# GLA states: gates projected first and values last, decays among the projections, sample outputs in four column tiles, sample states in two row tiles

## The chip, the core and the metric

The kernel runs on one core of one Trainium2 chip. Its engines are TensorE (PE, matmuls and the loads of their weights), VectorE (DVE), ScalarE (ACT) and GpSimd (POOL); SyncE (SP) issues most DMAs. Each engine works through its own list in order, and the engines meet at semaphores. The metric is the device time of one execution in microseconds (us).

## The reference

One inference step of a trunk of two layers on 512 prompt rows and 8 samples of 8 new rows (64 rows). Layer 0 mixes by attention, layer 1 by gated linear attention (GLA); each then has a feed-forward network with a short convolution. The change is in the mixer of layer 1, with 4 heads, dk = 128, dv = 256:

```python
def step(S, inp):                       # one chunk of one head
    qc, kc, vc, gc = inp
    b = jnp.cumsum(gc, axis=2)
    o_inter = jnp.einsum('bhtd,bhdv->bhtv', qc * jnp.exp(b), S)
    att = jnp.einsum('bhtd,bhsd,bhtsd->bhts', qc, kc, decay)      # decay = exp(b_t - b_s), s <= t
    o = o_inter + jnp.einsum('bhts,bhsv->bhtv', att, vc)
    S = jnp.exp(b_last) * S + jnp.einsum('bhsd,bhsv->bhdv', kc * jnp.exp(b_last - b), vc)
    return S, o
h = x @ w_in                            # q | k | v | r
on = o * lax.rsqrt(jnp.mean(jnp.square(o), -1, keepdims=True) + RMS_EPS) * norm_g
y = (on * jax.nn.silu(r)) @ w_out
```

The prompt starts from a zero state, each sample from its own (128 x 256 per head, read from HBM and written back). The outputs are y and the states.

## The kernel before, in words

The 576 rows are five tiles: four of 128 prompt rows (t = 0 to 3) and one of the 64 sample rows (t = 4). Each weight is loaded in units of 512 KB by SP into `raw`; ACT rounds a unit (`split_hi`, L1138), DVE takes the rest (`split_lo`, L1475), and PE forms three products per weight tile (`project`, L669 and L680 for the sample tile). In layer 1, q and k come first, feature-major, with the decays' cumulative sums `g_b`; then eight units `gla_vr` project the values v (units 0 to 3) and then the gates r (units 4 to 7), each unit in five steps, one per tile. Beside these 40 steps run 32 level steps (4 heads x 8 levels, L1026 and L1032 on PE), which build the decayed scores `att[h]`: DVE makes differences (`differences`), ACT their exponentials (`decay`), DVE the decayed q and k (`decayed`), PE the products (`level_products`) and DVE places them by mask (`placed`, L1857). DVE works one level step ahead of PE.

Then comes the stage of states, head by head, behind the last projection:

- ACT takes the exponentials of the sums (`decays_of`), DVE scales keys and queries (`prepare`, L1904, L1905), PE turns the scaled keys in five transposes (`turn_keys_of`, L650), ACT copies them out. For head 0 this is done after the last projection, for head h + 1 during head h. ACT applies SiLU to all five gate tiles (L1432) ahead of head 0's squares.
- PE forms four prompt state increments (L1059, 128 rows), then four prompt outputs: `att` times values (L1074) and, from tile 1 on, scaled queries times the state before (L1078). DVE carries the state (`bring_state`, L1934 and L1941), ACT squares each output (L1441) and DVE multiplies it by the gate (`gate_out`, L1926).
- The samples: one product of scores and values (L1088), then eight matmuls that add each sample's queries times its state. The queries of sample s stand in a block of 64 columns that is zero outside its own eight (`g_qz`), so each of the eight takes 64 columns of the array and all add into the same 64 rows of PSUM (L1090). Then eight state increments (L1059, 64 rows): the keys are zeroed outside the sample (`g_kz`, L1916). DVE adds each to the decayed old state (L1978).
- POOL stores the states (L2084, L2086). The sample states of the heads take turns in two buffers: SP loads head 2's when head 0's has been stored, head 3's when head 1's has.
- In the last head, DVE takes the reciprocal of all roots and then norms and scales every piece (`normed`, L1949), two tiles before its last four state updates and three between the y tiles; PE turns y (`turn_y`, L650), ACT and DVE copy it out in two parts (`take_x` L1124, `x_los` L1482), and PE starts the output projection (`gla_out`, L669).

The order on each engine is written out by hand. What holds PE in the loop of heads are these waits:

```python
            turn_keys_of(0)
            for h in range(GH):
                pe.wait_ge(turned_out, BATCH_GLA + 2 * h + 2)
                ...
                for s in range(SEQS):
                    mm = pe.matmul(place, g_qz[par][:, s, :], g_sst[par][:, s, :], start=False, stop=s == SEQS - 1)
                mm.then_inc(go_done, 1)
                for s in range(SEQS):
                    if s == 4 and h + 1 < GH:
                        turn_keys_of(h + 1)
                    state_product(h, PQ + s, g_kz[par][0:NS, s, :], vv)
```

## Time and profile before

| | us |
|---|---|
| median of 3 runs (lowest, highest) | 1608.63 (1607.99, 1610.58) |
| the profiled execution | 1606.65 |
| its span, first to last instruction | 1604.9 |
| PE busy in the span (share) | 1508.3 (94%) |
| DVE busy | 920.0 (57%) |
| ACT busy | 553.4 (34%) |
| POOL busy | 57.1 (4%) |
| granted TensorE clock, mean | 0.971 |

### The profile page before, as it was taken

Reading aid. Unit: us, or ns where it says so; the run is one execution under the profiler, and the core shown is the slowest. Engines: PE = TensorE matmul, PEld = TensorE weight load, DVE = VectorE, ACT = ScalarE, POOL = GpSimd, SP = SyncE. Lnnn points to the kernel's source line nnn. Section 1 sums busy time; section 2 is a strip of 40 time slices with the busy share of each in tenths; the row PEclk is TensorE's granted clock in tenths of the full one; section 3 lists DMA queues with packets and bytes.
Section 4 is the critical chain, followed back from the end, with each engine's and each line's share of the span. In section 5 each row is a group of like instructions: output and inputs, shape, how many; then the busy total and the mean of one; then the engine's idle time right before and its main releaser. Section 6 shows DMA issues by size and latency. Waiting matters only on the chain.

```text
span 1604.9 us, 24203 instructions
## 1 busy us (share of the span) xinstructions
PE 1508.3 (94%) x9372; PEld 1331.2 (83%) x9372; DVE 920.0 (57%) x1738; ACT 553.4 (34%) x1030; POOL 57.1 (4%) x90
## 2 busy tenths in 40 slices
PE   6999897889999999999799999899899999999995
PEld 5888675669999999878698888668799999998784
DVE  2654253377666666554721776575676666665545
ACT  3222276324333333332225332521243333333321
POOL 0002200010000000000100000000100000000000
PEclk9999999989999999999899999999799999999998
DMA  5225456622223321422211211442022333214211
GB/s 174 102 99 163 115 203 232 171 73 80 79 82 90 88 80 52 129 79 92 78 55 53 79 53 53 136 150 80 27 80 79 84 90 87 79 52 128 79 66 59
DMA packets 153215, 153.56 MB, mean 96 GB/s; under 512 B 12014, under 2 KB 122734, under 8 KB 152910
## 3 DMA queue, kind: packets, MB, share of 16 engines
q1 hardware_dynamic: 149210, 139.47, 28.1%
q0 software_dynamic: 3936, 13.14, 2.6%
q8 instruction: 47, 0.77, 0.2%
q14 instruction: 22, 0.18, 0.0%
HBM read 140.76 MB, written 21.91 MB: 101 GB/s over the span
## 4 chain that ended last, share of the span: by engine, by line
PE 85%; DVE 7%; ACT 3%; SPq 2%; issue 2%; DMA 1%; POOL 0%; ACTq 0%; DVEq 0%; POOLq 0%
PE ps L669 69%; PE ps L680 4%; PE ps L650 4%; PE ps L1026 1%; DVE x_reg L1684 1%; PE ps L737 1%; PE ps L1059 1%; PE ps L771 1%; SPq L522 1%; PE ps L1090 1%; DVE x_reg L1688 1%; DVE w_lo L1475 1%; ACT w_hi L1138 1%; PE ps L947 1%; DVE x_reg L1666 1%
## 5 line engine op out<-in xcount | busy, mean ns | idle before, releaser
L669 PE MATMUL ps<-xh_reg,w_hi 128*128 128x288 f32 x1552 | 465.4, 300 | 8.2 <-DVE xl_reg L1482 8.2
L669 PE MATMUL ps<-xl_reg,w_hi 128*128 128x288 f32 x1552 | 460.8, 297 | 0.0
L669 PE MATMUL ps<-xh_reg,w_lo 128*128 128x288 f32 x1552 | 460.8, 297 | 0.0
L669 PE MATMUL ps<-w_hi,xh_reg 128*128 128x512 f32 x768 | 308.2, 401 | 6.9 <-DVE xl_reg L1726 3.4
L669 PEld LDWEIGHTS ps<-xh_reg,w_hi 128*128 128x128 f32 x1552 | 295.1, 190 | 10.5 <-DVE xl_reg L1482 5.4
L669 PE MATMUL ps<-w_hi,xl_reg 128*128 128x512 f32 x768 | 302.2, 394 | 0.0
L669 PE MATMUL ps<-w_lo,xh_reg 128*128 128x512 f32 x768 | 302.1, 393 | 0.0
L669 PEld LDWEIGHTS ps<-xl_reg,w_hi 128*128 128x128 f32 x1552 | 295.3, 190 | 0.0
L669 PEld LDWEIGHTS ps<-xh_reg,w_lo 128*128 128x128 f32 x1552 | 294.9, 190 | 0.0
L1475 DVE TENSOR_TENSOR w_lo<-raw,w_hi 128x2048 fp32r<-128x2048 f32 (+1 forms) x52 | 113.7, 2186 | 259.1 <-ACT w_hi L1138 259.1
L669 PEld LDWEIGHTS ps<-w_hi,xh_reg 128*128 128x128 f32 x768 | 146.3, 191 | 39.0 <-issue 7.2
L1138 ACT ACTIVATE w_hi<-raw 128x2048 fp32r<-128x2048 f32 (+1 forms) x55 | 100.8, 1833 | 223.2 <-PE ps L680 215.0
L669 PEld LDWEIGHTS ps<-w_hi,xl_reg 128*128 128x128 f32 x768 | 145.9, 190 | 31.4
L1761 DVE TENSOR_SCALAR arena<-arena 128x512 f32<-128x512 f32 (+1 forms) x176 | 67.7, 427 | 179.3 <-ACT arena L1297 179.3
L1763 DVE SCALAR_TENSOR_TENSOR arena<-arena 128x512 f32<-128x512 f32 x352 | 166.8, 515 | 6.3
L669 PEld LDWEIGHTS ps<-w_lo,xh_reg 128*128 128x128 f32 x768 | 146.3, 191 | 28.9
L1296 ACT ACTIVATE arena<-ps 128x224 f32<-128x224 f32 x88 | 31.5, 358 | 239.4 <-PE ps L669 239.4
L1745 DVE TENSOR_TENSOR w_lo<-raw,w_hi 128x2048 fp32r<-128x2048 f32 x44 | 100.5, 2284 | 3.3 <-ACT w_hi L1283 3.1
L1283 ACT ACTIVATE w_hi<-raw 128x2048 fp32r<-128x2048 f32 x44 | 83.7, 1902 | 0.1
L680 PE MATMUL ps<-w_hi,xh_reg 128*128 128x512 f32 x192 | 75.8, 395 | 1.3 <-DVE x_reg L1670 1.3
L650 PE MATMUL ps<-ident,x_reg 128*128 128x128 f32 (+1 forms) x232 | 40.9, 335 | 38.1 <-DVE xl_reg L1482 12.2
L1294 ACT ACTIVATE arena<-ps 128x288 f32<-128x288 f32 x88 | 36.0, 412 | 112.7 <-PE ps L669 112.7
(188 smaller groups left out, 1530.5 us busy)
## 6 DMA issues: line engine op xcount, KB each, us to landing
raw<-in_ffn_w_up SPq DMA_DIRECT2D x88, 512.0 KB, 5.0
raw<-in_ffn_w_down SPq DMA_DIRECT2D x40, 512.0 KB, 4.6
raw<-in_attn_w_in SPq DMA_DIRECT2D x24, 512.0 KB, 4.8
raw<-in_gla_w_in SPq DMA_DIRECT2D x24, 512.0 KB, 4.6
out_swa_s<-in_state_swa_kv SPq DMA_DIRECT2D x2, 3968.0 KB
x_reg<-in_x_prompt SPq DMA_DIRECT2D x8, 512.0 KB, 7.1
raw<-in_gla_w_out SPq DMA_DIRECT2D x8, 512.0 KB, 4.7
out_swa_p<-arena POOLq DMA_DIRECT2D x18, 128.0 KB, 3.0
```

Of the source, the lines that this page charges most:

```text
L522: sp.dma_start(values_of[s][:, b:b + GROUP_BLOCKS[g], :] if g < 3 else values_of[s][:, b, :], src).then_inc(v_cached[s // 4], 16)
L650: last = pe.transpose(ps[0:cols, bank, col:col + rows], src, ident[0:rows, 0:rows])
L669: mm = pe.matmul(out, lhs(i, a), rhs(i, b), start=first and i == 0 and a + b == 0, stop=last and i == ks - 1 and a == 1)
L680: mm = pe.matmul(ps[:, t, :], xTh[:, k0 + i, NP:SLOT], w[b][:, i, :], start=first and i + b == 0, stop=last and i == kn - 1 and b == 1)
L1138: act.activation(w_hi[:, n % 2, 0:a], raw[:, n % 2, 0:a], ACT.Copy).then_inc(hi_done, 1)
L1283: act.activation(w_hi[:, slot, :], raw[:, slot, :], ACT.Copy).then_inc(hi_done, 1)
L1294: act.activation(ext[:, u, v, 2:2 + SPLIT], ps[:, m, 0:SPLIT], ACT.Copy).then_inc(ext_ready, 1)
L1296: act.activation(ext[:, u, v, 2 + SPLIT:2 + NP], ps[:, m, 0:PRE], ACT.Copy)
L1475: dve.tensor_tensor(w_lo[:, n % 2, 0:a], raw[:, n % 2, 0:a], w_hi[:, n % 2, 0:a].bitcast(F32), ALU.subtract).then_inc(lo_done, 1)
L1745: dve.tensor_tensor(w_lo[:, slot, :], raw[:, slot, :], w_hi[:, slot, :].bitcast(F32), ALU.subtract).then_inc(lo_done, 1)
L1761: ins = dve.tensor_scalar(y, e, w, fj[:, u, v, SIDE - 1:SIDE], ALU.mult, ALU.add)
L1763: ins = dve.scalar_tensor_tensor(y, e, w, y, ALU.mult, ALU.add)
```

## The change

The projection order becomes gates first, values last. With that, ACT applies SiLU during the last unit. For heads 0 to 2, the differences, exponentials and scalings (in place, in `g_k` and `g_q`) and the key transposes go in between the level steps, one head after its eight levels; the transposes are in two parts, three and two. Head 3's scalings stand after the last level, followed by a product of each gate tile with the norm's weights (`norm_gate`); its transposes stand behind head 0's prompt states on PE. The decays at chunk ends are taken once for all heads (`ends`).

A sample's queries now stand in a block of 32 columns (four samples share one), and the eight sample outputs go to four column tiles of the array and so to four groups of 32 PSUM rows, two matmuls each; ACT copies the lower 64 rows (`o_low`), DVE adds the upper ones and multiplies by the gate. A state increment reads only 32 rows of keys and values, in row tile 0 or 1, which alternate and write to alternating banks; PSUM places are handed out in groups of four. Roots and reciprocals are taken per head, and the scaling by them is on ACT (`scale_by_root`), a head later. The sample states have places of their own except head 2, which follows head 0. The low part of the second `gla_out` unit goes from DVE to POOL.

```diff
+KEYS_AT = [(h_ + 1) * (NLEV + 1) for h_ in range(GH)]
+LAST_ENDS_AT = LEVEL_STEPS - 5
...
+        g_state = [cut(arena, 24592 + i * GV, GV) for i in range(2)]
         g_sst = [x.rearrange("p (s n) -> p s n", s=SEQS)
-                 for x in (cut(gla_side, 7296, SEQS * GV), cut(arena, 21560, SEQS * GV))]
-        squares = cut(gla_side, 9344, GV)
+                 for x in (cut(arena, 21560, SEQS * GV), cut(gla_side, 7680, SEQS * GV), cut(arena, 21560, SEQS * GV),
+                           cut(arena, 17152, SEQS * GV))]
...
-                k0, kn, c0, cn = c % 2 * 4, 4, (c // 2 + (2 if kind == "gla_vr" else 0)) * HALF, HALF
+                k0, kn, c0, cn = c % 2 * 4, 4, ((c // 2 + 2) % 4 + 2 if kind == "gla_vr" else c // 2) * HALF, HALF
...
             for h in range(GH):
                 if h == 0:
+                    sp.wait_ge(lev_prod, GH * LEV_ALL)
+                elif h == 1:
                     sp.wait_ge(steps, STEPS_BEFORE[out])
-                elif h == 1:
-                    sp.wait_ge(lev_prod, GH * LEV_ALL)
+                elif h == 2:
+                    sp.wait_ge(s_state_out[0], 16)
                 else:
-                    sp.wait_ge(s_state_out[h % 2], 16)
-                sp.dma_start(g_sst[h % 2], io["state_gla"][0, :, h].rearrange("s d v -> d s v")).then_inc(gla_state_in[h % 2], 16)
+                    sp.wait_ge(go_done, 2 * NTILE)
+                sp.dma_start(g_sst[h], io["state_gla"][0, :, h].rearrange("s d v -> d s v")).then_inc(gla_state_in[h], 16)
                 if h == 1:
                     load_unit(out + 2)
                     load_unit(out + 3)
...
+            def turn_keys_of(h, part):
...
+                if part == 0:
+                    for c in range(3):
+                        mm = pe.transpose(ps[:, 7, NS + c * P:NS + (c + 1) * P], g_k[:, h, c * P:(c + 1) * P], ident[:, :])
+                else:
+                    pe.transpose(ps[:, 7, NS:NS + P], g_k[:, h, 3 * P:NP], ident[:, :])
+                    mm = pe.transpose(ps[0:NS, 7, NS + P:NS + 2 * P], g_k[:, h, NP:NT], ident[:, :])
+                mm.then_inc(keys_turned, 1)
...
+                    for h in range(GH - 1):
+                        for part in range(2):
+                            if m == KEYS_AT[h] + 4 + part:
+                                turn_keys_of(h, part)
+            pe.wait_ge(tok_read, 3 * NTILE + PQ)
             pe.wait_ge(lev_read, GH * LEV_ALL)
...
             for h in range(GH):
                 par = h % 2
-                pe.wait_ge(turned_out, BATCH_GLA + 2 * h + 2)
+                pe.wait_ge(keys_taken, 2 * h + 2)
                 for c in range(PQ):
-                    state_product(h, c, g_kt[par][:, c, :], g_v[:, c, h * GV:(h + 1) * GV])
+                    state_product(h, c, keys_of(h)[:, c, :], g_v[:, c, h * GV:(h + 1) * GV])
+                if h == 0:
+                    turn_keys_of(GH - 1, 0)
+                    turn_keys_of(GH - 1, 1)
+                pe.wait_ge(q_scaled, h + 1)
                 for c in range(PQ):
                     n = h * NTILE + c
-                    if n >= 3:
-                        pe.wait_ge(go_read, n - 2)
...
                     place = head_out_place(n, P)
                     mm = pe.matmul(place, att[h][:, c * P:(c + 1) * P], g_v[:, c, h * GV:(h + 1) * GV],
                                    start=True, stop=c == 0)
                     if c >= 1:
                         pe.wait_ge(gs_read, h * HEAD_STEPS + c)
-                        mm = pe.matmul(place, g_qb[par][:, c * P:(c + 1) * P], g_state[(c - 1) % 2],
+                        mm = pe.matmul(place, g_q[:, h, c * P:(c + 1) * P], g_state[(c - 1) % 2],
                                        start=False, stop=True)
                     mm.then_inc(go_done, 1)
...
-                pe.matmul(place, att[h][0:NS, NP:NT], vv, start=True, stop=False)
-                for s in range(SEQS):
-                    mm = pe.matmul(place, g_qz[par][:, s, :], g_sst[par][:, s, :], start=False, stop=s == SEQS - 1)
+                pe.matmul(place[0:NS], att[h][0:NS, NP:NT], vv, start=True, stop=False, skip_group_check=True)
+                for b in range(2):
+                    for s in (b, 4 + b, 2 + b, 6 + b):
+                        at = 32 * (s // 4) + NS * (s % 4 // 2)
+                        mm = pe.matmul(place[at:at + 32], g_qz[par][:, s, :], g_sst[h][:, s, :], start=at >= NS and b == 0, stop=b == 1,
+                                       skip_group_check=True, tile_position=(0, at))
                 mm.then_inc(go_done, 1)
-                for s in range(SEQS):
-                    if s == 4 and h + 1 < GH:
-                        turn_keys_of(h + 1)
-                    state_product(h, PQ + s, g_kz[par][0:NS, s, :], vv)
+                pe.wait_ge(kz_ready, h + 1)
+                for i in range(PQ, HEAD_STEPS):
+                    s = sample_of(i)
+                    rows = slice(32 * (s // 4), 32 * (s // 4) + 32)
+                    state_product(h, i, g_kz[par][rows, s % 4, :], vv[rows])
...
+                    for h in range(GH):
+                        if m == (KEYS_AT[h] if h < GH - 1 else LAST_ENDS_AT + 1):
+                            decays_of(h)
+                        for part in range(2):
+                            if h < GH - 1 and m == KEYS_AT[h] + 5 + part:
+                                take_keys_of(h, part)
...
+                    if i == 7 and t < 3:
+                        if t == 0:
+                            act.wait_ge(tok_read, 3 * NTILE)
+                        for tile in range(2 * t, min(2 * t + 2, NTILE)):
+                            silu_of(tile)
...
+                for t in range(PQ):
+                    act.wait_ge(go_done, h * NTILE + t + 1)
+                    square(h, t, head_out_place(h * NTILE + t, P))
+                act.wait_ge(go_done, (h + 1) * NTILE)
+                if h:
+                    act.wait_ge(go_read, h * NTILE)
+                act.activation(o_sum_of[0:NS, :], head_out_place(h * NTILE + PQ, NS), ACT.Copy).then_inc(o_low, 1)
+                if h:
+                    scale_by_root(h - 1)
+                else:
                     split_hi(UNIT_NO[("gla_out", 1)])
...
+                act.wait_ge(o_summed, h + 1)
+                square(h, PQ, o_sum_of[0:NS, :])
+                act.wait_ge(sq_done, sq.n)
+                act.activation(g_rs[:, :, h], g_ss[:, :, h], ACT.Sqrt, bias=eps_ln[:, 1:2], scale=1.0 / GV).then_inc(roots, 1)
+            scale_by_root(GH - 1)
+            act.wait_ge(gs_done, GH * HEAD_STEPS // 2)
...
+            def scale_keys(h):
+                dve.wait_ge(lev_prod, levels_done((h + 1) * (NLEV + 1) - 1))
+                dve.wait_ge(decays, 2 * h + 2)
+                dve.tensor_tensor(g_k[:, h], g_k[:, h], to_end, ALU.mult).then_inc(keys_ready, 1)
+            def scale_queries(h):
+                dve.tensor_tensor(g_q[:, h], g_q[:, h], from_start, ALU.mult).then_inc(q_scaled, 1)
+            def norm_gate(t):
+                n = TILES[t][1]
+                dve.wait_ge(r_gate, t + 1)
+                r = g_r[0:n, t, :].rearrange("p (h v) -> p h v", h=GH)
+                dve.tensor_tensor(r, r, g_norm[0:n, :].rearrange("p (o v) -> p o v", o=1).to_broadcast([n, GH, GV]),
+                                  ALU.mult).then_inc(r_normed, 1)
...
+                        if m == (KEYS_AT[h] - 1 if h < GH - 1 else LAST_ENDS_AT):
+                            end_differences(h)
+                        if h < GH - 1 and m == KEYS_AT[h] + 1:
+                            scale_keys(h)
+                        if h < GH - 1 and m == KEYS_AT[h] + 2:
+                            scale_queries(h)
             placed(LEVEL_STEPS - 1)
+            scale_keys(GH - 1)
+            scale_queries(GH - 1)
+            for t in range(NTILE):
+                norm_gate(t)
...
-                dve.wait_ge(sq_done, n + 1)
                 if h == 0:
-                    dve.wait_ge(r_gate, t + 1)
+                    dve.wait_ge(r_normed, t + 1)
                 r = g_r[0:rows, t, h * GV:(h + 1) * GV]
-                dve.tensor_tensor(r, head_out_place(n, rows), r, ALU.mult).then_inc(go_read, 1)
+                if t < PQ:
+                    dve.wait_ge(sq_done, n + 1)
+                    dve.tensor_tensor(r, head_out_place(n, rows), r, ALU.mult).then_inc(go_read, 1)
+                    return
+                dve.wait_ge(o_low, h + 1)
+                dve.tensor_tensor(o_sum_of[0:NS, :], head_out_place(n, P)[NS:P], o_sum_of[0:NS, :], ALU.add).then_inc(o_summed, 1)
+                dve.wait_ge(o_summed, h + 1)
+                dve.tensor_tensor(r, o_sum_of[0:NS, :], r, ALU.mult).then_inc(go_read, 1)
+            def place_samples(h):
...
+                for a in range(2):
+                    ins = dve.tensor_copy(g_qz_own[par][a], g_q[:, h, NP + 32 * a:NP + 32 * a + 32].rearrange("p (s t) -> p s t", s=4))
+                ins.then_inc(qz_own, 1)
+                dve.wait_ge(keys_taken, 2 * h + 2)
+                dve.tensor_tensor(g_kz[par][0:NS, :, :], sample_keys_of(h).rearrange("p (s d) -> p s d", s=1).to_broadcast([NS, 4, P]),
+                                  row_in_four.rearrange("p (s o) -> p s o", o=1).to_broadcast([NS, 4, P]), ALU.mult).then_inc(kz_ready, 1)
...
             add_low_half_of_vr(3)
-            prepare_samples(0)
+            place_samples(0)
             for h in range(GH):
                 for c in range(PQ):
                     bring_state(h, c)
                     if c >= 1:
                         gate_out(h, c - 1)
+                gate_out(h, 3)
                 if h + 1 < GH:
-                    prepare(h + 1)
-                gate_out(h, 3)
+                    place_samples(h + 1)
                 gate_out(h, 4)
...
+                def root(h):
+                    dve.wait_ge(roots, h + 1)
+                    dve.reciprocal(g_rs[:, :, h], g_rs[:, :, h]).then_inc(rs_ready, 1)
+                if h == GH - 1:
+                    root(h)
+                for i in range(PQ, HEAD_STEPS):
+                    n, s = h * HEAD_STEPS + i, sample_of(i)
+                    if i == PQ:
                         dve.wait_ge(go_done, (h + 1) * NTILE)
+                    dve.wait_ge(gs_done, 2 * (n // 4 + 1))
+                    state = g_sst[h][:, s, :]
+                    dve.scalar_tensor_tensor(state, state, ends[:, h, PQ + s:PQ + s + 1], state_place(n),
                                              ALU.mult, ALU.add).then_inc(gs_read, 1)
...
-                if h == 0:
-                    split_lo(UNIT_NO[("gla_out", 1)])
+                if h < GH - 1:
+                    root(h)
+            dve.wait_ge(s_state_out[1], 16)
...
                 pool.dma_start(io["gla_p"][0, 0, h], g_state[1]).then_inc(p_state_out, 16)
+                if h == 0:
+                    n = UNIT_NO[("gla_out", 1)]
+                    pool.wait_ge(hi_done, n + 1)
+                    pool.wait_ge(lo_done, n)
+                    pool.tensor_tensor(w_lo[:, n % 2, 0:UNIT], raw[:, n % 2, 0:UNIT], w_hi[:, n % 2, 0:UNIT].bitcast(F32),
+                                       ALU.subtract).then_inc(lo_done, 1)
                 pool.wait_ge(gs_read, (h + 1) * HEAD_STEPS)
-                pool.dma_start(io["gla_s"][0, :, h].rearrange("s d v -> d s v"), g_sst[h % 2]).then_inc(s_state_out[h % 2], 16)
+                pool.dma_start(io["gla_s"][0, :, h].rearrange("s d v -> d s v"), g_sst[h]).then_inc(s_state_out[h], 16)
```

## Rows read from the trace of the kernel before

**Rows 1.** The page, chain that ended last: shares of the span by engine.

```profile
PE 85%; DVE 7%; ACT 3%; SPq 2%; issue 2%; DMA 1%; POOL 0%; ACTq 0%; DVEq 0%; POOLq 0%
```

**Rows 2.** Windows: stretch, length, busy time (instructions) per engine, PEclk, DMA share, GB/s.

```profile
970.00:1012.60 42.60, 42.04 (x230) 35.50 (x228) 23.59 (x47) 13.06 (x18) 0.00 (x0) 1.00 0.08 26
1017.00:1020.00 3.00, 3.00 (x7) 2.46 (x8) 1.98 (x3) 2.99 (x3) 0.00 (x0) 0.50 1.10 353
295.00:300.00 5.00, 5.00 (x58) 2.71 (x58) 0.03 (x1) 1.07 (x4) 0.00 (x0) 1.00 0.04 11
```

**Rows 3.** PE's timeline, end of projections to output projection: start, length, line, shapes, records [idle].

```profile
1012.42 0.39 PE L680 MATMUL ps<-w_lo,xh_reg 128*128 128x512 f32 x1
1015.32 1.01 PE L650 MATMUL ps<-ident,gla_side 128*128 128x128 f32 x5 [2.50 <-DVE arena L1538]
1082.51 0.78 PE L669 MATMUL ps<-w_hi,xh_reg 128*128 128x512 f32 x1
```

**Rows 4.** Chain of waits in the stage of states: start, length, what (records).

```profile
1018.21 4.84 ACT arena L1432 x5
1051.45 0.86 PE ps L1074 x4
1054.47 0.57 PE ps L1088 x2
1055.04 3.60 PE ps L1090 x16
1058.64 1.92 PE ps L1059 x8
1061.26 3.85 PE ps L1059 x16
1065.10 0.86 PE ps L1074 x4
1075.34 3.26 DVE arena L1949 x8
```

**Rows 5.** PE's timeline in layer 0's attention: column tiles, next line, row tiles.

```profile
295.41 1.07 PE L845 MATMUL ps<-v_cache_reg,arena 128*32 128x256 f32 x16
296.41 1.56 PE L840 MATMUL ps<-arena 64*128 64x256 f32 x6
200.07 1.99 PE L737 MATMUL ps<-arena 64*128 64x512 f32 x8
```

**Rows 6.** DVE in the stage: line, shapes, count | busy, mean ns | idle before.

```profile
L1978 DVE SCALAR_TENSOR_TENSOR gla_side<-gla_side,arena,ps 128x256 f32<-128x256 f32 x16 | 6.8, 477 | 2.2 <-PE ps L1059 2.2
L1926 DVE TENSOR_TENSOR arena<-ps,arena 128x256 f32<-128x256 f32 x16 | 6.7, 422 | 3.8 <-ACT gla_side L1441 3.8
L1916 DVE TENSOR_TENSOR gla_side<-gla_side,arena 64x1024 f32<-64x1024 f32 x4 | 4.8, 1212 | 1.7 <-ACT gla_side L1124 1.7
```

**Rows 7.** DVE's timeline: the first instruction behind its last level.

```profile
1008.58 0.81 DVE L1895 TENSOR_TENSOR arena<-arena 128x512 f32<-128x512 f32 x2
```

**Rows 8.** ACT from the last unit on, columns as in 6.

```profile
L1441 ACT ACTIVATE gla_side<-ps 128x256 f32<-128x256 f32 x16 | 6.1, 379 | 14.0 <-PE ps L1074 9.0 <-PE ps L1078 4.8
L1138 ACT ACTIVATE w_hi<-raw 128x2048 fp32r<-128x2048 f32 x2 | 3.8, 1907 | 3.0 <-PE ps L680 3.0
L1441 ACT ACTIVATION_READ_ACCUMULATOR gla_side<-ps 128x1 f32 x16 | 3.1, 194 | 0.0
L1448 ACT ACT_TABLE_LOAD x1 | 1.3, 1283 | 0.0
```

**Rows 9.** Timelines of POOL and DVE behind layer 0's second norm.

```profile
784.92 4.79 POOL L2052 TENSOR_TENSOR w_lo<-raw,w_hi 128x2048 fp32r<-128x2048 f32 x1 [126.99 <-ACT w_hi L1138]
786.95 3.84 DVE L1684 SCALAR_TENSOR_TENSOR x_reg<-x_reg,ln_mv,arena 128x1024 f32<-128x1024 f32 x1
```

**Rows 10.** DMA issues in the stage: what, queue, KB each, us to landing.

```profile
out_gla_s<-arena POOLq DMA_DIRECT2D x1, 1024.0 KB, 5.1
gla_side<-in_state_gla SPq DMA_DIRECT2D x1, 1024.0 KB, 5.6
```

More of the change, by code:

```diff
@@ L281, in build_program @@
         att = [cut(arena, at, NT) for at in (18304, 18880, 20064, 20640)]
-        from_start = [lev_e[:, i] for i in range(2)]
+        from_start = cut(arena, 24592, NT)
         to_end = cut(arena, 24016, NT)
+        ends = cut(arena, 21216, GH * (PQ + SEQS)).rearrange("p (h n) -> p h n", h=GH)
         lev_q = cut(arena, 21560, 2 * NT).rearrange("p (b n) -> p b n", b=2)
@@ L430, in state_place, with sample_of @@
         def state_place(n):
-            return ps[:, n // 2 % 3, n % 2 * GV:n % 2 * GV + GV]
+            j = n % 4
+            bank, part = (j // 2, j % 2) if n % HEAD_STEPS < PQ else (j % 2, j // 2)
+            return ps[:, n // 4 % 2 * 2 + bank, part * GV:part * GV + GV]
+        def sample_of(i):
+            return (i - PQ) // 2 + 4 * ((i - PQ) % 2)
         def head_out_place(n, rows):
-            return ps[0:rows, (3, 4, 7)[n % 3], 0:GV]
+            return ps[0:rows, (5, 6, 7, 4)[n % 4], 0:GV]
         def h_count(l, c, t):
@@ L1044, in _ @@
                         level_products(m)
-            pe.wait_ge(tok_read, 4 * NTILE)
+                    for h in range(GH - 1):
[3 more added lines that the diff above has]
+            pe.wait_ge(tok_read, 3 * NTILE + PQ)
             pe.wait_ge(lev_read, GH * LEV_ALL)
-            def turn_keys_of(h):
-                pe.wait_ge(kz_ready, 3 * h + 1)
-                turn([(c * P, g_kb[h % 2][:, c * P:(c + 1) * P]) for c in range(PQ)])
-                turn([(0, g_kb[h % 2][:, NP:NT])])
             def state_product(h, i, lhs, rhs):
                 n = h * HEAD_STEPS + i
-                if n >= 6 and n % 2 == 0:
+                if n >= 8 and n % 4 == 0:
                     pe.wait_ge(gs_read, n - 4)
@@ L1428, in _ @@
-            take_keys_of(0)
-            act.wait_ge(tok_read, 4 * NTILE)
-            for t in range(NTILE):
-                n = TILES[t][1]
-                act.activation(g_r[0:n, t, :], g_r[0:n, t, :], ACT.Silu).then_inc(r_gate, 1)
-            for h in range(GH):
-                for t in range(NTILE):
-                    if t == 3 and h + 1 < GH:
-                        decays_of(h + 1)
-                    n = TILES[t][1]
-                    act.wait_ge(go_done, sq.n + 1)
-                    if sq.n >= 1:
-                        act.wait_ge(sq_done, sq.n)
-                    act.activation(squares[0:n, :], head_out_place(sq.n, n), ACT.Square,
-                                   accum_out=g_ss[0:n, t, h:h + 1]).then_inc(sq_done, sq.one())
-                if h + 1 < GH:
-                    take_keys_of(h + 1)
-                if h == 0:
-                    split_hi(UNIT_NO[("gla_out", 1)])
@@ L1447, in _, with square @@
-            act.wait_ge(sq_done, GH * NTILE)
-            act.activation(g_rs.rearrange("p t h -> p (t h)"), g_ss.rearrange("p t h -> p (t h)"), ACT.Sqrt,
-                           bias=eps_ln[:, 1:2], scale=1.0 / GV).then_inc(gates, 1)
-            act.wait_ge(p_state_out, 16 * GH)
-            act.wait_ge(s_state_out[0], 32)
+            take_keys_of(GH - 1, 0)
+            take_keys_of(GH - 1, 1)
+            def square(h, t, src):
+                n = TILES[t][1]
+                if sq.n >= 1:
+                    act.wait_ge(sq_done, sq.n)
+                act.activation(squares[0:n, :], src, ACT.Square, accum_out=g_ss[0:n, t, h:h + 1]).then_inc(sq_done, sq.one())
@@ L1919, in gate_out @@
+            placed(LEVEL_STEPS - 1)
+            scale_keys(GH - 1)
+            scale_queries(GH - 1)
+            for t in range(NTILE):
+                norm_gate(t)
             def gate_out(h, t):
@@ L1937, in bring_state @@
                     dve.wait_ge(go_done, h * NTILE + c)
+                if h == 0 and c == 1:
+                    dve.wait_ge(ends_ready, 1)
                 if c == 1 and h:
@@ L1959, in _ @@
                         gate_out(h, c - 1)
+                gate_out(h, 3)
                 if h + 1 < GH:
-                    prepare(h + 1)
-                gate_out(h, 3)
+                    place_samples(h + 1)
                 gate_out(h, 4)
-                for s in range(SEQS):
-                    n = h * HEAD_STEPS + PQ + s
-                    if h == GH - 1 and s == 4:
-                        dve.wait_ge(gates, 4)
-                        dve.reciprocal(g_rs, g_rs).then_inc(vec, vs.one())
-                        settle()
-                        dve.wait_ge(go_read, GH * NTILE)
-                        normed(0)
-                        normed(1)
-                    if s == 0:
+                def root(h):
+                    dve.wait_ge(roots, h + 1)
+                    dve.reciprocal(g_rs[:, :, h], g_rs[:, :, h]).then_inc(rs_ready, 1)
@@ L2100, in _ @@
             pool.wait_ge(p_state_out, 16 * GH)
-            for i in range(2):
-                pool.wait_ge(s_state_out[i], 32)
+            for h in range(GH):
+                pool.wait_ge(s_state_out[h], 16)
             for i in range(ROPED):
```

194 lines of the change are left out of this document (110 added, 84 removed).

## The prediction

> **What bounds the kernel now.** I read the chain of waits first: PE carries 85% of it [rows 1], so the time is what PE does plus what PE waits for. Then the windows, for where PE is not fed. In the last third of the GLA projections it is busy 42.04 of 42.60 us at the granted clock 1.00, while DVE has 23.59 us of work [rows 2]: what is put beside PE there is nearly free, what is put on PE costs. Right behind comes the stage that the diff rebuilds. I call the start of the last projection matmul plus its 0.39 us E = 1012.81; the first matmul of the output projection starts at 1082.51 [rows 3]. These 69.7 us hold the four heads; before E and after that matmul PE's own list stays, but for some transposes. So the question is the length of this stage, and what the projections pay for work moved into them.
>
> The chain inside the stage [rows 4] has three parts. At its head stand ACT's five SiLUs (4.84 us), which end at 1023.05, 10.2 us after E, before ACT reads the first outputs; here the clock is at 0.50, its lower level (1.2 GHz), after PE had waited 2.50 us [rows 2, 3]. Later heads are pure PE: the row of four output matmul records comes at 1051.45 and again at 1065.10, a period of 13.65 us. In it the eight sample outputs take 3.60 us, and the eight sample states 1.92 plus half of the 3.85 us row. At the end, after PE's last matmul, DVE norms and scales eight pieces (3.26 us) before y can be turned.
>
> **Part 1, sample products on a part of the array.** The eight sample outputs become 32 columns wide in four column tiles. The attention stage has this shape: 8 matmuls 128x32 by 256 columns (16 records) start at 295.41 and the next line at 296.41, so 1.00 us [rows 5]. I take 1.00 for 3.60. The sample states become 32 rows in two row tiles, in alternating banks. The nearest row is two 64-row tiles: 4 matmuls of 512 columns in 1.99 us [rows 5], as many columns as 8 of 256. So 1.9 us for 3.85; the other end is no overlap, 3.85. PE per head is then 3.1 (outputs) + 0.6 (scores times values) + 1.0 + 1.9 + 1.9 (prompt states) = 8.5 us, the key transposes gone elsewhere.
>
> **Part 2, who paces a head then.** DVE does; I follow its order from the first state copy (B). Copy, three state updates and three gates are tied to PE's output matmuls: 3.0 us, as in [rows 4] from 1051.45 to 1054.47. The fourth gate waits for the fourth output and its square on ACT: B+3.9. Placing the next head's samples is two small copies and a 64x512 product, half of the 1.21 us row [rows 6], 0.85 in all: B+4.7. The sample gate waits for PE's sample outputs (B+4.5) and ACT's copy of the lower rows, then takes two instructions near 0.42 us [rows 6]: B+5.8. Eight state updates of 0.477 [rows 6], overlapping at their ends to 0.41 as the eight in 3.26 us do [rows 4]: B+9.1. A small reciprocal: B+9.4, the next head's copy. So 9.4 us a head, and PE waits some 0.9 us for DVE to free the banks. Gone from DVE are two 576-column scalings, half of the sample keys, and head 0's weight split, which goes to Pool. ACT's list per head (five squares of 0.38 plus a read of 0.19 each [rows 8], five scalings and a copy of 256 columns at about 0.38, a root) sums to 5.4 us and stays beneath. Bounds for the period: 8.5 (PE alone) and, with no overlap in either tiling, 8.5 + 2.6 + 1.95 = 13.05.
>
> **Part 3, the start.** Decays, key scaling and SiLU are done in the projections, so PE goes on at E with the first states, without the pause after which the clock fell. But DVE is late. It ends its last level at 1008.58, E-4.2 [rows 7]. Then come two scalings of head 3, by columns 0.73 each: E-2.8; five norm gates of 1024 columns, at 1.21 less the overlap of 0.07, E+2.9; the late half of the values, E+3.5; head 0's samples, E+4.4 = B0. PE's own list (states 1.9, head 3's five transposes with ACT's copies between) ends near E+3.2, so the transposes are covered; without DVE's delay they would cost 1.3.
>
> **Part 4, the state buffers.** The states of heads 0, 1 and 3 get places that come free early. Head 2 still waits until head 0's is stored. That store is on Pool's queue behind the new weight split: ACT copies head 0's lower rows at E+8.9 and then rounds that unit in 1.9 [rows 8], to E+11.2; Pool's split takes 4.79 [rows 9]: E+16.0, though DVE is done at E+13.5. Store 5.1 and load 5.6 [rows 10]: E+26.7. Head 2 wants it at E+4.4+18.8+3.0 = E+26.2. So 0.5 us; bounds 0 and, with both transfers half as slow again, 5.9. Head 3's load is behind it on SP's queue and is wanted 9 us later; gate and bias of the norm, issued later than now, have some 30 us until their use.
>
> **Part 5, the end.** In the last head DVE takes the root ahead of the eight updates: ACT's squares, the scalings of head 2 and the root end at B+7.3, the reciprocal at B+7.6, the updates at B+10.9. ACT's scalings of head 3 run beside them; the first turned y is copied by B+10.2, its low part made at B+12.1, the second tile's transposes end at B+13.1. First projection: B+13.2. The 3.26 us of norms are gone from this path.
>
> **Part 6, what the projections pay.** Fifteen transposes of heads 0 to 2 go onto PE there; five took 0.70 among the states (1060.56 to 1061.26 [rows 4]). In two pieces a head I take 0.73: 2.2 us, bounds 1.6 and 5 (a step lost at each unit's start). DVE gets some 7 us more over the three heads, where the windowed third alone has 19 us free; a level step is prepared one step ahead, which covers it. If that cover failed, PE would wait for one instruction, 0.7 us, each time. ACT's exponentials, key copies, SiLUs and their table load lie in its idle time.
>
> **Sum.** B0 = E+4.4, three periods 28.2, transfer 0.5, end 13.2: E+46.3 against E+69.7, so 23.4 saved; minus 2.2 gives 21.2. The profiled execution took 1606.65 us (span 1604.9); 1606.65 - 21.2 = 1585.4. The median of the runs shown is 1.98 above it, so 1587.4.
>
> **A rule that speaks against it.** Beside Pool's split at 784.92, a 1024-column DVE product from SBUF took 3.84 us, until 790.79, 1.1 after Pool's end [rows 9], against 1.21 for that size [rows 6]. The Trainium skill (SBUF — State Buffer, "SBUF: two separate sides") says that DVE and GpSimd share a port pair as an exclusive lock, which a DVE instruction with two SBUF inputs meets while GpSimd reads SBUF; the trace agrees. Here the split falls on E+11.2 to E+16.0, where DVE runs updates that take one operand from PSUM; its last product from SBUF alone, the sample gate, is done by E+10.2. I charge nothing; were DVE a microsecond late, up to 4.8 us.
>
> **Rivals.** (a) The tiles don't overlap, so the change doesn't do what it says: at 13.05 a head, 3 x 3.65 + 3 at the end = 14 back, 1601. For: 32-row tiles are nowhere in this trace. Against: the column row is of the very shape. (b) Each head has a root between squares, and a table load is 1283 ns [rows 8]. Squares ran after SiLU and after the exponential with no load of their own; the root had one. If root and square load in turn, the next head's first gate is late by 0.7 three times and the last root by 1.3: some 4, so 1591. The Trainium skill (ScalarE: Activation LUTs, "Table sets: the hidden batching unit") advises to batch by set, and names copy, not square, as filler of every set; no run here shows it for the root's set. (c) State transfers pace head 2: 5.4 more, 1593; with the lock as well, 1597. (d) Slower: the granted clock falls to its lower level through the heads, since each now holds waits and tiles that fill a quarter of the array. PE per head doubles to 17; E+4.4 + 51 + 13.2 + 4 (the last head's sample products) is E+72.6, with 2.2 slower by 5.1: 1614. It decides from 16 us a head on. For: 0.50 at 1017 to 1020. Against: the stretch of column tiles, 295 to 300, had 1.00 [rows 2]. (e) DVE is early everywhere and PE alone paces: 3 less and no transfer wait, 1584. (f) No change: a and c together, 1607.
>
> **Chances.** Forecast (1582 to 1591, with e) 0.62; b or c 0.20; a 0.11; f 0.03; d 0.04. The range leaves out d, f and a: 1581 to 1598. 0.2% (3.2 us) is about what can be told from no change: faster 0.93, same 0.03, slower 0.04.
>
> **What would show it.** Eight sample outputs in 1.0 us and eight states in 1.9; a period of 9.4 between first state copies, ended by DVE's updates; the first copy 4.4 after E; no SiLU and no 0.50 clock behind E; Pool's split between heads 0 and 1; the stage 46 us long. Wrong would be: PE rows of 3.6 us again, a head waiting for the state's DMA, table loads in each head, or projections longer by more than 5 us.

## The result, and the profile after

The kernel takes 1593.45 us (median of 4 runs, 1591.91 to 1594.55) where the kernel before takes 1609.35; the ratio is 0.9903, 95% interval 0.9891 to 0.9916. That is 15.9 us gained, 21.2 were forecast. 1593.45 lies inside the range (1581 to 1598), but outside the 1582 to 1591 that had a chance of 0.62. The profiled execution took 1592.71 us (span 1590.9). PE still carries the chain:

```profile
PE 84%; DVE 7%; ACT 3%; issue 2%; SPq 2%; DMA 2%; POOL 0%; ACTq 0%; DVEq 0%; POOLq 0%
```

PE's timeline of the changed kernel, with the columns of [rows 3]. L1054 is a level step's products; L697 and L708 are projections, L1103 the states, L1144 the sample outputs, L1140 the sample scores times values ahead of them, L678 transposes of y.

```profile
893.04 1.16 PE L1054 MATMUL ps<-arena 128*128 128x128 f32 x8 [0.16 <-DVE arena L1931]
...
1015.95 0.39 PE L708 MATMUL ps<-w_lo,xh_reg 128*128 128x512 f32 x1
...
1024.13 1.07 PE L1144 MATMUL ps<-arena,gla_side 128*32 128x256 f32 x16
1025.14 2.00 PE L1103 MATMUL ps<-arena,gla_side 32*128 32x256 f32 x16
1028.46 1.97 PE L1103 MATMUL ps<-arena 128*128 128x256 f32 x8 [1.33 <-DVE arena L2088]
...
1038.21 3.54 PE L1103 MATMUL ps<-arena 128*128 128x256 f32 x8 [1.26 <-DVE gla_side L2088]
...
1046.22 0.61 PE L1140 MATMUL ps<-arena 64*64 64x256 f32 x2 [1.45 <-DMA arena<-in_state_gla]
...
1047.76 3.38 PE L1103 MATMUL ps<-arena,gla_side 32*128 32x256 f32 x16
1051.34 3.75 PE L1103 MATMUL ps<-arena 128*128 128x256 f32 x8 [0.20 <-DVE arena L2088]
...
1063.72 1.09 PE L678 MATMUL ps<-ident,arena 128*128 128x128 f32 x8 [2.06 <-ACT arena L1520]
1067.12 1.94 PE L678 MATMUL ps<-ident,arena 128*128 128x128 f32 x8 [2.31 <-DVE xl_reg L1570]
1068.72 0.78 PE L697 MATMUL ps<-w_hi,xh_reg 128*128 128x512 f32 x1
```

E is now 1015.95 + 0.39 = 1016.34, and the stage of states 1068.72 - 1016.34 = 52.4 us, against 69.7 before [rows 3] and 46.3 forecast. The sample outputs take 1.07 for 3.60 and the sample states 2.00 for 3.85 where the row is undisturbed. But three rows of states, two of the prompt and one of the samples, take 3.4 to 3.75, nearly twice their time. The same stage on DVE's timeline: the first state copy of each head (L2052), head 0's eight sample updates (L2088), the last root's reciprocal (L2078).

```profile
1020.73 0.42 DVE L2052 COPY arena<-ps 128x256 f32<-128x256 f32 x1
...
1026.66 3.22 DVE L2088 SCALAR_TENSOR_TENSOR arena<-arena,ps 128x256 f32<-128x256 f32 x8
...
1029.90 0.39 DVE L2052 COPY arena<-ps 128x256 f32<-128x256 f32 x1
...
1040.30 0.42 DVE L2052 COPY arena<-ps 128x256 f32<-128x256 f32 x1 [0.56 <-PE ps L1103]
...
1053.43 0.42 DVE L2052 COPY arena<-ps 128x256 f32<-128x256 f32 x1 [0.49 <-PE ps L1103]
...
1062.93 0.19 DVE L2078 RECIPROCAL arena<-arena 128x5 f32<-128x5 f32 x1 [1.85 <-ACT arena L1537]
```

So head 0's first state copy (B0) comes at E+4.39, the periods between the heads' first copies are 9.17, 10.40 and 13.13, and from the last of them to the output projection (the end) it is 15.29. Windows of the changed kernel, columns as in [rows 2], show why: PEclk, the number behind the five engines, falls to 0.50 twice in the heads, and once more in the end.

```profile
1027.14:1028.46 1.32, 0.00 (x0) 0.03 (x1) 1.32 (x5) 1.30 (x4) 0.92 (x1) 1.00 0.00 0
1037.50:1038.00 0.50, 0.00 (x0) 0.00 (x0) 0.50 (x3) 0.47 (x3) 0.00 (x0) 0.98 1.03 418
1038.00:1041.00 3.00, 2.79 (x7) 2.29 (x8) 2.30 (x8) 0.19 (x1) 0.90 (x1) 0.50 0.69 256
1041.50:1048.00 6.50, 5.05 (x36) 3.37 (x36) 3.33 (x9) 2.00 (x9) 0.55 (x1) 1.00 0.93 328
1048.50:1055.00 6.50, 6.30 (x23) 4.55 (x20) 4.95 (x13) 2.47 (x8) 0.90 (x1) 0.50 0.44 159
1065.00:1069.00 4.00, 1.88 (x9) 1.91 (x10) 2.70 (x7) 1.82 (x4) 0.90 (x1) 0.54 0.22 78
```

PE waits 1.33 us ahead of head 1, 1.26 ahead of head 2 and 1.45 inside it. In windows of 0.1 us the clock goes to its lower level (1.2 GHz) at 1038.0, 0.2 ahead of the end of the second wait, and at 1048.2, when PE has worked again for 2.0 us behind the third. The fall in the end lasts from 1065.3 to about 1072 and begins within PE's wait of 2.31 us, which follows one of 2.06. The third wait is for head 2's states; these rows are Pool's split with the store queued behind it, then SP's load:

```profile
1027.54 4.54 POOL L2202 TENSOR_TENSOR w_lo<-raw,w_hi 128x2048 fp32r<-128x2048 f32 x1 [3.30 <-ACT w_hi L1194]
1032.02 0.94 POOL L2205 DMA_DIRECT2D out_gla_s<-arena  x1
```

```profile
1039.94 0.99 SPq L651 DMA_DIRECT2D arena<-in_state_gla  x2
```

### The profile page after: what moved, and what is told of

Read it like the earlier page. It is cut to its first block, busy times and chain, and to the rows that moved or that the text cites. A ratio compares the mean times of both kernels' runs of the same rounds, so it can differ in the third digit from the quotient of the medians.

```text
span 1590.9 us, 24255 instructions
## 1 busy us (share of the span) xinstructions
PE 1491.3 (94%) x9372; PEld 1319.9 (83%) x9372; DVE 915.5 (58%) x1734; ACT 562.5 (35%) x1062; POOL 61.2 (4%) x91
## 4 chain that ended last, share of the span: by engine, by line
PE 84%; DVE 7%; ACT 3%; issue 2%; SPq 2%; DMA 2%; POOL 0%; ACTq 0%; DVEq 0%; POOLq 0%
PE ps L697 69%; PE ps L708 5%; PE ps L678 4%; PE ps L1054 1%; DVE x_reg L1772 1%; PE ps L765 1%; PE ps L799 1%; SPq L549 1%; DVE x_reg L1776 1%; ACT w_hi L1194 1%; DVE w_lo L1563 1%; PE ps L975 1%; DVE x_reg L1754 1%; DVE ln_stats L1761 1%; DVE xl_reg L1570 1%
## 5 line engine op out<-in xcount | busy, mean ns | idle before, releaser
L697 PE MATMUL ps<-xh_reg,w_hi 128*128 128x288 f32 x1552 | 465.4, 300 | 8.2 <-DVE xl_reg L1570 8.2
L697 PE MATMUL ps<-xl_reg,w_hi 128*128 128x288 f32 x1552 | 460.8, 297 | 0.0
L697 PE MATMUL ps<-xh_reg,w_lo 128*128 128x288 f32 x1552 | 460.7, 297 | 0.0
L697 PE MATMUL ps<-w_hi,xh_reg 128*128 128x512 f32 x768 | 309.5, 403 | 6.9 <-DVE xl_reg L1814 3.4
L697 PEld LDWEIGHTS ps<-xh_reg,w_hi 128*128 128x128 f32 x1552 | 294.9, 190 | 10.5 <-DVE xl_reg L1570 5.4
L697 PE MATMUL ps<-w_lo,xh_reg 128*128 128x512 f32 x768 | 303.1, 395 | 0.0
L697 PE MATMUL ps<-w_hi,xl_reg 128*128 128x512 f32 x768 | 303.0, 395 | 0.0
L697 PEld LDWEIGHTS ps<-xl_reg,w_hi 128*128 128x128 f32 x1552 | 295.1, 190 | 0.0
L697 PEld LDWEIGHTS ps<-xh_reg,w_lo 128*128 128x128 f32 x1552 | 294.6, 190 | 0.0
L697 PEld LDWEIGHTS ps<-w_hi,xh_reg 128*128 128x128 f32 x768 | 146.6, 191 | 39.0 <-issue 7.2
L697 PEld LDWEIGHTS ps<-w_hi,xl_reg 128*128 128x128 f32 x768 | 146.5, 191 | 31.6
L697 PEld LDWEIGHTS ps<-w_lo,xh_reg 128*128 128x128 f32 x768 | 147.0, 191 | 29.0
L678 PE MATMUL ps<-ident,x_reg 128*128 128x128 f32 (+1 forms) x232 | 41.0, 336 | 39.2 <-DVE xl_reg L1570 11.3
L708 PE MATMUL ps<-w_hi,xh_reg 128*128 128x512 f32 x192 | 75.9, 395 | 1.3 <-DVE x_reg L1758 1.3
```

What stands on the lines that cost most here:

```text
L678: last = pe.transpose(ps[0:cols, bank, col:col + rows], src, ident[0:rows, 0:rows])
L697: mm = pe.matmul(out, lhs(i, a), rhs(i, b), start=first and i == 0 and a + b == 0, stop=last and i == ks - 1 and a == 1)
L708: mm = pe.matmul(ps[:, t, :], xTh[:, k0 + i, NP:SLOT], w[b][:, i, :], start=first and i + b == 0, stop=last and i == kn - 1 and b == 1)
```

## The experiments

Theories: the clock (PE's short waits bring the granted clock down), the transfer (head 2's states), DVE's chain being longer than worked out, and narrow tiles, not waits, lowering the clock. "Stage" is from E to the first output projection, out of each profile; the times are medians, with their own runs of the kernel before (1608.1 to 1608.7). A profiled execution lies up to 2 us from its median, so stages and times are each compared with their like.

**x1_again: the changed kernel again.** 

> The changed kernel once more, unedited. Its profile had periods between first state copies of 9.17, 10.40 and 13.13 us and 52.4 us from the last projection to the first output projection, with the granted clock at 0.50 in two stretches (about 1038.0 to 1041.3 and 1048.1 to 1055.0). If the falls of the clock belong to the kernel, the same two stretches come again, each within half a microsecond of the same instruction, and the stage is 52.4 within 1 us. If they are chance, the periods move by more than 1 us.

Stage 52.43, periods 9.17, 10.40, 13.23; the same two falls in the heads at the same instructions; 1593.8 us. They belong to the kernel.

**x2_store_first.** On Pool:
```
 pool.dma_start(gla_s h = 0)      # moved ahead of
 pool.tensor_tensor(w_lo split)
```

> Only the order of two steps on Pool is changed: head 0's sample states are stored ahead of the weight split, so the store is issued about 2.1 us earlier (1029.9 for 1032.0) and head 2's states land about 1044 for 1046.2. Transfer theory (the wait for head 2's states is what costs, and the clock falls at 1048.1 because of that wait): PE's 1.45 us wait goes, the third period drops from 13.1 to between 9.4 and 10.4, the end from 15.3 to about 13.5, in all 4 to 5 us less. Clock theory (any short waits of PE bring the clock down, this one or another): the wait goes, 1.5 us less, but a stretch of 0.50 stays in head 2 or 3 and the third period stays above 11. Chain theory (DVE's list is simply longer than worked out): under 0.5 us less.

The wait for head 2's states is gone, yet the stage is 52.6, with periods of 9.17, 11.32 and 12.58 (1591.44 us; by the intervals of the two ratios this is not told from x1's time). Pool's split then lay beside head 1's sample placing. DVE's two small copies and Pool's split in this run:

```profile
1034.29 1.47 DVE L2038 COPY gla_side<-arena 128x32 f32<-128x32 f32 x2
```

```profile
1031.07 4.56 POOL L2204 TENSOR_TENSOR w_lo<-raw,w_hi 128x2048 fp32r<-128x2048 f32 x1
```

The copies take 0.26 elsewhere; here they end 0.1 after the split (1035.63). PE then waits 2.19 ahead of head 2, the clock falls for longer (from 1038 to 1044.8), and a second fall follows around its wait of 1.26 ahead of head 3. The Trainium skill (SBUF — State Buffer, "SBUF: two separate sides") has this lock, held for a whole instruction, and counts copies from SBUF to SBUF in fp32 among what meets it; this run agrees with 1.2 us.

**x3_warm.**
```
+ if h + 1 < GH:
+     for _ in range(3): pe.matmul(next head's output place, ident, g_v[:, 0, 0:256])
```

> Three matmuls of 128x256 that nobody reads (about 1.4 us at full clock) are put between the heads, where PE waits 1.26 to 1.33 us for DVE. Clock theory: the row of prompt states of head 2 takes 1.9 to 2.0 us for 3.54, the second period goes from 10.4 to about 9.4; the third still holds the transfer wait, and is 11 to 13; in all 1 to 5 us less. Transfer theory: the second period improves by about 1, the third and the end stay at 13.1 and 15.3, 1 us less. If the clock falls for the narrow tiles and not for the waits, the stretches of 0.50 stay and the stage is 0 to 0.5 us longer by the added matmuls.

The second period is 9.75 and its clock 1.00, as the clock theory has it. But PE reaches head 2's samples earlier and the states land at the same time, so the wait there is longer, and the clock falls behind it:

```profile
1029.28:1039.03 9.75, 9.75 (x64) 7.21 (x63) 8.29 (x23) 4.97 (x17) 3.60 (x3) 1.00 0.62 223
1039.03:1054.95 15.92, 12.81 (x62) 9.24 (x61) 8.44 (x24) 4.97 (x17) 2.36 (x3) 0.79 0.68 226
```

The wait is 3.11 us, the stage 53.6, the time 1593.25. Neither cure works alone; the expected ceiling of 13 for that period and the gain of 1 to 5 us were misses.

**x4_whole_array: part 1's overlap taken away.**
```
- at = 32 * (s // 4) + NS * (s % 4 // 2)
+ at = 0
- rows = slice(32 * (s // 4), 32 * (s // 4) + 32)
+ rows = slice(0, NS)
```

> Part 1 undone in its timing: all eight sample outputs of a head go to one column tile, and the eight sample states use all 64 rows, so nothing runs side by side; the sample outputs and states are then not the reference's. PE per head grows by 2.6 and 1.9 us to about 13. If part 1 is worth what was counted, the periods become 12.6 to 13.2 each and the stage 58 to 63 us, 6 to 10 us more than the changed kernel. PE then hardly waits: by the clock theory no 0.50 stretch is left before the last head, and by a theory of narrow tiles too. If DVE or the transfers set the length anyway, the stage grows by less than 3 us.

Periods 12.41, 12.95, 12.96, stage 59.1, 1598.14 us. PE's rows, and a window of one head:

```profile
1036.61 3.64 PE L1144 MATMUL ps<-gla_side 128*32 128x256 f32 x16
1040.18 3.72 PE L1103 MATMUL ps<-arena,gla_side 64*128 64x256 f32 x16
```

```profile
1045.60:1058.56 12.96, 12.78 (x58) 8.88 (x57) 8.37 (x23) 4.97 (x17) 1.46 (x2) 1.00 0.54 191
```

Side by side the tiles save 2.6 and 1.7 us a head. PE waits only 0.18 between the heads here and the clock stays at 1.00 in all of them. So the overlap is worth 6.7 us of stage in the changed kernel (4.7 by the medians), and 11.9 against y2 below, where the clock is held (10.7 by the medians; y2 has the split moved as well).

**y1_split_late.** Pool's split goes behind the store of head 2; on SP `load_unit(out + 3)` goes behind the state loads. 

> Pool's weight split goes behind the store of head 2's sample states (beside head 3, where DVE has one instruction that works on SBUF alone), and the load of the fourth output unit goes behind the state loads on SP's queue, since it waits for that split. So head 0's store goes out at about E+13.8 (E is the end of the last projection matmul), as in the run with the store first, but no split lies beside head 1. Lock theory (in that run two copies of DVE took 1.47 us for 0.26 because Pool's split held the port): the copies take 0.26 again and PE's wait ahead of head 2 is 1.26 for 2.19. The transfer wait is gone. Clock theory: the clock still falls after the 1.26 us waits ahead of heads 2 and 3, so the periods are 9.2, 10.4 and about 10.4, the end about 15, and the stage 49 to 50 us against 52.4. If the transfer wait was the whole cause, the third period is 9.4, the end 13.3, the stage 46.7. If neither counts, 52.

Stage 48.7, periods 9.17, 10.39, 10.66, end 14.11; 1588.88 us. The copies take 0.26 again and no state is waited for. PE's rows of states ahead of heads 2 and 3:

```profile
1038.40 3.52 PE L1103 MATMUL ps<-arena 128*128 128x256 f32 x8 [1.26 <-DVE gla_side L2088]
...
1049.70 1.97 PE L1103 MATMUL ps<-arena 128*128 128x256 f32 x8 [1.26 <-DVE arena L2088]
```

Of the two falls in the heads the second is gone with the transfer wait, though PE waits 1.26 ahead of head 3 too; I had expected it to fall there.

**y2_split_late_warm.** y1 and x3 together. 

> The same with three unread matmuls of 128x256 between the heads. Clock theory with the transfer theory together: no stretch of 0.50 is left between E and the last head's end, the periods are 9.2, 9.4 to 9.8 and 9.4 to 9.8, the end 13.3 to 14.4, the stage 46.5 to 48 us, 4.5 to 6 less than the changed kernel, which is the forecast stage of 46.3. If the clock falls for narrow tiles, it still falls in heads 2 or 3 and the stage stays near 49.5.

```profile
1030.67:1040.42 9.75, 9.75 (x64) 7.21 (x63) 8.28 (x24) 4.97 (x17) 1.47 (x2) 1.00 0.67 225
1040.42:1050.16 9.74, 9.74 (x64) 7.20 (x63) 8.28 (x23) 4.97 (x17) 1.45 (x2) 1.00 0.67 234
```

Stage 47.15 (4.38 + 28.66 + 14.11), 1587.47 us: in the heads narrow tiles, no waits, clock 1.00 (it falls in the end, at PE's wait of 2.06 us ahead of y's transposes). The forecast stage was 46.3. Against y1 only the unread matmuls are new, so narrow tiles without waits don't bring the clock down here, and DVE's chain being longer explains at most the 0.9 us that is left. Whether the tiles add to what the waits do, no run separates.

**y4_early: norm gates and last root earlier.**
```
+ EARLY_GATES = {-2: (0, 1), -1: (2, 3, 4)}   # DVE, by level steps counted from the last
- scale_by_root(2) after head 3's outputs       # ACT
+ scale_piece(2, t) after each square of head 3
```

> The changed kernel with only the early norm gates and the scalings of head 2 between the squares of head 3; the split, the transfers and the waits of PE as in the changed kernel. The first state copy at E+2.3 for E+4.4; the wait for head 2's states and both falls of the clock move with it and stay, so the periods stay 9.2, 10.4 and 13.1; the end is 13.4 for 15.3. Stage 48.4, 4 us less. If the wait of head 2 is tied to the projections and not to the heads, it grows by 2.1 and the gain is 2 us.

B0 is E+2.15 and the end 12.47, as expected. Head 0's period grew to 10.54, since DVE now waits 0.99 for ACT's first square, and the clock fell ahead of head 1 instead of head 2. The wait for head 2's states, expected to stay, is gone, and so is the second fall. So the periods are 10.54, 11.16 and 10.00, not those expected; stage 46.3 for 48.4 expected, 1587.83 us.

**y3_all and z1_best.** y2 and y4, with unread matmuls around y's first transposes as well; z1 has two for three between the heads and one for four ahead of the transposes. 

> The kernel before this in the list, plus: DVE's five norm gates between its last two level steps instead of behind them, ACT's scalings of head 2 put one by one behind the squares of head 3 so that the last root doesn't wait for them, and four unread matmuls ahead of and four behind the first transposes of y. By the steps of the sum: the first state copy at E+2.3 for E+4.4 (then ended by the late half of the values and by placing head 0's samples), the end shorter by the 1.85 us that DVE waits for the last root, the first output projections at full clock. Stage 42 to 44 us, in all 9 to 12 us less than the changed kernel, about 1582. If the norm gates are not what holds the first copy, it stays at E+4.4 and the gain is 2 us smaller; if the end is set by DVE's updates and not by the root, it stays at 13.5.

 

> The kernel with everything (split late, unread matmuls, early norm gates, early root) with the fill cut to the waits: two unread matmuls between the heads for three, one ahead of the first transposes of y for four. With three the heads' period was PE's own 9.75 us, DVE's pace being 9.2. If two still hold the granted clock at 1.00: periods 9.2 to 9.5, the first transposes of y about 1 us earlier behind the last head's states, the stage 42 to 43 us for 44.1, the time 1 to 2 us below that kernel's, near 1583.5. If the clock falls again: a 0.50 stretch in heads 1 to 3 and a stage of 45 us or more.

Stages 44.1 and 44.0, 1585.04 and 1582.41 us, no 0.50 anywhere in the stage; z1's ratio to the kernel before is 0.9842 (0.9829 to 0.9855), 11 us below the changed kernel's 1593.45. z1's windows of heads 1 to 3:

```profile
1029.40:1039.14 9.74, 9.54 (x62) 6.82 (x61) 8.28 (x23) 4.97 (x17) 1.47 (x2) 1.00 0.67 226
1039.14:1048.89 9.75, 9.55 (x62) 6.83 (x61) 8.28 (x24) 4.97 (x17) 1.46 (x2) 1.00 0.67 235
1048.89:1061.00 12.11, 11.48 (x78) 8.23 (x76) 8.89 (x22) 8.44 (x25) 6.85 (x4) 1.00 0.66 240
```

With a third of the fill gone the period is the same, so it isn't the fill that sets it: the expected 9.2 to 9.5 missed, 9.75 is the pace of PE and DVE together. The stage missed its 42 to 43 as well. As the two stages are the same, the 2.6 us between the two medians don't come from it, and the intervals of the two ratios overlap; that less fill is faster is not shown.

**z2_silu_late: the gates' SiLUs back behind the projections.**
```
- silu_of(tile)                        # among the last projections
+ for tile in range(NTILE): silu_of(tile)   # behind take_keys_of(GH - 1, 1)
```

> The changed kernel with one part undone: ACT's five SiLUs of the gates run behind the projections and behind head 3's key copies, as the kernel before had them late, with DVE's norm gates behind them. By the steps of the sum: table load 1.28 and SiLUs 5.2 from E+3.6 on, the last norm gate done at about E+11.3, the first state copy at about E+12.8 for E+4.4; the later periods as in the changed kernel. Stage 60 to 62 us, 8 to 10 more than the changed kernel. If DVE's lateness at the start is taken up later (by the wait for head 2's states, which would then have landed), the third period is about 10.4 to 11 for 13.1 and the stage 57 to 59.

```profile
1022.69 5.76 DVE L1982 TENSOR_TENSOR arena<-arena 128x1024 f32<-128x1024 f32 x5 [8.81 <-ACT arena L1469]
...
1029.97 0.42 DVE L2052 COPY arena<-ps 128x256 f32<-128x256 f32 x1
```

B0 is E+13.29, the stage 65.2 where 60 to 62 or less was expected, 1605.29 us: most of the gain is gone. 8.9 of the 12.8 us are the start; the rest is the clock at 0.50 after PE's 9.76 us wait and a transfer wait of 3.12 (I expected that wait to shrink).

**z3_turn_twice: the fifteen key transposes in the projections issued twice.** 

> The fifteen key transposes that the changed kernel issues among the projections are issued twice. From the first level step to the end of the last projection the kernel before took 121.59 us and the changed one 123.30. If those 1.71 us are the transposes' own time on PE, it becomes 124.9 to 125.1. If they come from PE waiting for DVE's added work or for ACT's copies, it stays within 0.5 of 123.3.

```profile
892.86 1.16 PE L1054 MATMUL ps<-arena 128*128 128x128 f32 x8 [0.81 <-DVE arena L1932]
...
1017.44 0.39 PE L708 MATMUL ps<-w_lo,xh_reg 128*128 128x512 f32 x1
...
1029.95 3.46 PE L1104 MATMUL ps<-arena 128*128 128x256 f32 x8 [1.33 <-DVE arena L2089]
```

From the first level step to E 124.97 us: 1.67 more for fifteen more. Yet this single run took 1591.18 us and its stage 49.6. In the heads the clock fell ahead of head 1 instead of head 2, once instead of twice. PE came to head 2's samples at E+28.4 as in the changed kernel, but their states had landed at E+29.2 for E+29.9, so that wait was 0.89.

## Why the prediction was right in kind and 5.3 us off in size

- **Where the gain stands.** By the profiles 1606.65 - 1592.71 = 13.9. Of that the stage gives 17.3. The first level step starts 1.82 later than before (893.04 for 891.22), and PE is as late already in layer 0 (791.74 for 789.81), ahead of any part of the change; in the twelve profiles of the changed kernel and its variants that step starts between 892.37 and 895.00, in the one of the kernel before at 891.22, and why stays open. From there to E it takes 123.30 for 121.59, 1.71 more; behind the stage nothing differs (522.2 for 522.4). Without the 1.82 the change is worth 15.8, close to the medians' difference of 15.9. The step in the kernel before:

```profile
891.22 1.16 PE L1026 MATMUL ps<-arena 128*128 128x128 f32 x8
```

- **Part 1 right:** 1.07 and 2.00 where 1.00 and 1.9 were taken, and PE 8.5 a head.
- **Part 2, the period, short:** 9.4 forecast, 9.17 and, with the clock held, 9.75 and 9.74 measured. The list of DVE holds (8.3 us busy), and in head 0 the fourth gate ends at B+3.94 for B+3.9, its wait of 0.44 for ACT's square counted. Not counted was that in the later heads DVE waits 0.50 for the first square too: PE starts a head's states only when DVE's updates have freed the banks, so its first output comes later behind the copy. In the changed kernel itself the rows of states of heads 1 and 2 start 9.75 apart (1028.46 and 1038.21). That y2's three periods sum to 28.66 for 28.2 is partly luck: head 0 is shorter than forecast, the others longer.
- **The step that failed** is rival (d)'s. I saw that PE would wait some 0.9 us a head, and priced a fall of the clock only through all heads, from 16 us a head on, at 0.04. It falls for single stretches, two in the heads, and the rows of states in them take up to 1.9 times as long: 3.54 for 1.97, 3.38 for 2.00, 3.75 for 1.97, 4.7 in all. The stretch of column tiles that I held against it [rows 2] has no waits of this kind. y2 without waits, and x4 with 0.18, have no fall in the heads; that there is no fall without the waits is shown, but not every such wait brings one (1.33 us ahead of head 1, and 1.26 in y1). Filling the one ahead of head 2 gave back 1.6 us (y1 to y2).
- **Part 4, the transfer, short:** Pool's split ended at E+15.7 (E+16.0 forecast). But the store, issued right behind, was seen by SP 7.9 us later, not 5.1: it shared the DMA engines with the load of the fourth output unit (two pieces of 512 KB, held until that split) and head 1's prompt state. In y1, where that load comes later, SP sees the store after 5.1 us (1030.38 to 1035.48). The states were there at E+29.9 for E+26.7. PE's 1.45 us is more than the 0.5 taken, and with the clock behind it the wait costs 3.7 (x1 to y1). This is rival (c) with part of (d). That the time comes out at (c)'s 1593 is luck: (c) put 5.4 us on the transfer alone. The 0.20 for b or c was too low for c.
- **Part 5, the end, short by 0.9 with the full clock in the heads:** 14.11 in y2. The reciprocal ends at B+8.5, not B+7.6, since ACT's list, root included, ends at B+8.3, not B+7.3. The scalings of head 2 (2.09 us) were counted in it; what was not is that ACT's squares come 0.6 later behind the copy than in head 0, as in Part 2. The other 0.4 was not traced. In the changed kernel the slow first states add 1.2 more.
- **Part 3 right to 0.01 (E+4.4), step by step:** the gates end at E+2.87, the late half of the values at E+3.6. **Part 6:** 2.2 forecast, 1.71 measured, and z3 shows that it is the transposes' own time.
- **Rival (b) refuted:** ACT has one load for the root, at 1027.87 (1.28 us), and none between later squares and roots. **The lock** was rightly charged nothing here; x2 shows it with Pool's split 3.6 us later.

The sum again: 4.0 from periods and transfer, 2.1 from the end, less 0.5 from the projections and 0.2 behind the stage, is 5.4 of miss.

## What to carry to other kernels

When an engine other than PE comes to set the pace, PE's short waits can be a cost by themselves, as those of 1.3 to 1.5 us were here: count each as a possible stretch at half clock, not as all or nothing, and try to fill it with unread matmuls that end just before the wait does. A wait for a transfer and a fall of the clock hide each other, so curing one alone may show nothing. Where two instructions only happen not to meet (Pool's split and DVE's copies), a move of a few us (3.6 in x2) makes them meet.

## What the hardware did that I had not expected

Waits of 1.26 and 1.45 us came with the lower clock for some 3 and 7 us, an equal one of 1.33 us did not, and 1.7 us more work ahead (z3), or a start 2.2 us earlier (y4), changed which one did. Nor does the fall come at one place: within the wait of 1.26 us, but 2.0 us behind the end of the one of 1.45, when PE was busy. What picks the wait stays open: no run here separates it. In the one run of z3, more work on PE went with a stage 2.8 us shorter.
